# A two-layer diffusion trunk: 40 of 48 modulation units go from TensorE's matmuls to GpSimd's multiplies and sums

## The chip, the cores and the metric

The kernel runs on one core of a Trainium2 chip. The metric is the device time of one launch in microseconds (us), the median of some runs. An engine here is one of TensorE (PE in the profile, its weight loads PEld), VectorE (DVE), ScalarE (ACT), GpSimd (POOL) and SyncE (SP, which issues transfers). Each has its own in-order stream of instructions, and the streams meet only at semaphores: a `wait_ge(sem, n)` holds its own engine, and everything behind it on that engine, until the count is reached.

## The reference, cut to what matters

A layer takes 128 context tokens and 512 latent tokens, each with its own conditioning vector, and computes

```
m = silu(cvec) @ w_mod[l] + b_mod[l]                 # 1024 -> 6 x 1024, for 2 vectors
sh1, sc1, g1, sh2, sc2, g2 = split(m, 6)
h = rmsnorm(x) * (1 + sc1) + sh1
q, k, v, bg, cg, xc = split(h @ w_in[l])             # 1024 -> 3072
x = x + g1 * (concat(diff_attention(q, k, v), rmsnorm(bg * dwconv3(cg * xc))) @ w_out[l])
h2 = rmsnorm(x) * (1 + sc2) + sh2
a, b = split(dwconv3(h2 @ w_up[l]))                  # 1024 -> 2 x 2816
x = x + g2 * ((silu(a) * b) @ w_down[l])
```

for two layers. The change touches only the first line. Per layer it is a product of two vectors (context and latent) with a matrix of 1024 x 6144, 25 MB in float32, so its arithmetic is small and its weights are a third of a layer's. Of the results, sh1 and sc1 are wanted at the layer's start, g1 at the output projection, sh2 and sc2 in front of the MLP, g2 at the first down projection.

## The kernel before, in words

**Tokens.** All 640 tokens (with padding, T = 644 columns) pass together; large products are cut into two halves of 322 columns. Each float32 weight is split into a rounded part (`w_hi`, written by ScalarE) and a rest (`w_lo`, a subtraction by VectorE or, for one unit of each layer, GpSimd), and each product is three matmuls: hi x hi, hi x lo, lo x hi. Weights are staged in `raw_all` (nine blocks of 128x512), which SP fills in an order of units. Before, that order (`load_order`) interleaves weight units ("split") with modulation units ("mod").

**Stages of a layer.** (1) Norm and the products q, k, v, in six weight units (`qkv_unit`, loops p and t). (2) 24 "conv halves" (`conv_half`), with the 20 attention rounds between them: scores, the softmax on ScalarE and VectorE, transposes and the product with v, which goes to PSUM bank 7. (3) The output projection, four units (`out_unit`). (4) A gap: sums of squares (`stat`), root, reciprocal, spreading over the partitions (`spread`), the scaled rows `hfull`, and their split. (5) The MLP: 22 gates in four chunks. Two gates are plain; each other gate (`up_gate`) is seven products by a Strassen-like scheme, whose sums of weight blocks are made by GpSimd: three SBUF-to-SBUF transfers that add (`add_block`) and one `tensor_tensor` per gate. After each chunk comes its part of the down projection (`down_chunk`).

**Modulation before.** A unit is 1024 x 256 of `w_mod`. Its sum (`mod_sum`) is eight float32 matmuls: the eight inner tiles are spread over the four 32-column groups of the array, with `cT` (the activated vectors) stationary and the weights moving. Two units fill bank 7. ScalarE copies that to `mod_row` (`rows`), TensorE turns it by four transposes (`mod_turn`), VectorE sums the four groups and adds the bias (`mod_post`). There are 48 units: 8 (`pre_load`, `pre_sum`) are layer 0's sh1 and sc1 and are the same before and after; the other 40 are placed one by one between matmuls of q, k, v, of the output projection (layer 0 only) and in the two gaps. Those 40 end in 20 turns.

**GpSimd before** issues a few small loads and stores (`kc`, `v`, `rope`, new_k, new_v), and works only from the gap on: the subtraction for unit `G_U + 1` (line 680), six small `tensor_scalar` on `hfull` (line 685) and the sums for the gates (lines 668 and 698).

Of the kernel before, what the change touches and what calls it, by code (L numbers as in the profile page):

```python
# [15 lines left out]
P = 128  # L16
# [48 lines left out]
MOD_LAYER = 24  # L65
MOD_RING = MOD_LAYER - 8
RAW_SLOT = (N_SPLIT + MOD_RING) // 2
RAW_PRE = 0
MOD_PRE_G, MOD_LAYER_G = MOD_PRE // 2, MOD_LAYER // 2

# [8 lines left out]
GAP_A = [10] * LAST + [6]  # L79


def load_order(l):

    mod = [("mod", j) for j in range(MOD_LAYER)]
    split = [("split", n) for n in range(N_SPLIT)]
    order = split[0:4]
    for h in range(2, 6):
        order += mod[2 * h:2 * h + 2] + split[h + 2:h + 3]
    order += split[8:14]
    if l == LAST:  # L90
        return order + split[14:18]
    for h in range(6, 9):
        order += mod[2 * h:2 * h + 2] + split[h + 8:h + 9]
    return order + mod[18:20] + split[17:18]


ORDER = [load_order(l) for l in range(DEPTH)]


def raw_of(l, n):  # L100

    return ORDER[l].index(("split", n))
# [93 lines left out]
def mod_bank(l, h):  # L196

    return 2 if l is not None and h == GAP_A[l] + 1 else MOD_BANK


def sum_bank(l, h):

    return 4 if l and h == 1 else mod_bank(l, h)
# [5 lines left out]
def hybrid_step(nc, x_prompt, x_sample, cache_k, cache_v, c_sample, c_ctx, w_mod, b_mod, norm1_g, w_in, q_norm_g,  # L209
# [3 lines left out]
    with ctx:  # L213
# [28 lines left out]
        mod_row = sb("mod_row", [P, 2 * UC])  # L242
        qkg = sb("qkg", [P, 2, DEPTH, HD])
# [55 lines left out]
        early_gap = ExitStack()  # L299
        mod_t = sb("mod_t", [P, 2, SLOT], scope=early_gap)  # L300
        early_gap.close()
        ht_hi = sb("ht_hi", [P, KH, 3, HALF], F32R, scope=mlp)
        ht_lo = sb("ht_lo", [P, KH, 3, HALF], F32R, scope=mlp)
        gap = ExitStack()
        mod_x = sb("mod_x", [P, 2, SLOT], scope=gap)
        gap.close()
# [66 lines left out]
        modq_full, v_in = [sem("modq_full%d" % u) for u in range(4)], sem("v_in")  # L373
        modx_full, modt_full = sem("modx_full"), sem("modt_full")
# [31 lines left out]
        def landed(l, r):  # L406
            return 32 * (RAW_PRE + r % 2) + l * (32 * RAW_SLOT) + 32 * (r // 2)
# [6 lines left out]
        w_mod_v = w_mod.rearrange("l (t p) n -> p (l t) n", p=P)  # L414


        @block.sync
        def _(sp):
# [37 lines left out]
            def first_mods(layer, us):  # L456

                for u in us:
                    sp.dma_start(mod_q[:, u, :].rearrange("p (t n) -> p t n", n=UC),
                                 w_mod_v[:, layer * KT:(layer + 1) * KT, (u + 8) * UC:(u + 9) * UC]  # L460
                                 ).then_inc(modq_full[u], 16)

            for l in range(DEPTH):
                def free_of_split(n):
                    sp.wait_ge(split_full[n % 2], usable(l, n))

                def free_of_mod(k):
# [21 lines left out]
                def mod_source(j):  # L489

                    return (l, j + 8) if j < 16 else (l + 1, j - 16)

                def mod_unit(j, slot):

                    layer, unit = mod_source(j)
                    load(slot, w_mod_v, layer * KT, KT, unit * UC, UC)

                def gap_first():  # L500

                    sp.wait_ge(o_read, ROUNDS * (l + 1))
                    for i in range(2):
                        layer, unit = mod_source(2 * GAP_A[l] + i)
                        sp.dma_start(mod_t[:, i, :].rearrange("p (t n) -> p t n", n=UC),
                                     w_mod_v[:, layer * KT:(layer + 1) * KT, unit * UC:(unit + 1) * UC]
                                     ).then_inc(modt_full, 16)

                def gap_second():

                    sp.wait_ge(mix_ready, MIXN * (l + 1))
                    for i in range(2):
                        layer, unit = mod_source(2 * GAP_A[l] + 2 + i)
                        sp.dma_start(mod_x[:, i, :].rearrange("p (t n) -> p t n", n=UC),
                                     w_mod_v[:, layer * KT:(layer + 1) * KT, unit * UC:(unit + 1) * UC]
                                     ).then_inc(modx_full, 16)

# [3 lines left out]
                for r in range(2, len(ORDER[l])):  # L521
                    before, j = ORDER[l][r - 2]
                    if l or r not in (3, 4):
                        free_of_split(j) if before == "split" else free_of_mod(j + 1)
                    kind, n = ORDER[l][r]
                    if l == 0 and r == 3:
                        sp.wait_ge(mod_used, 6)
                        first_mods(0, (0, 1))
                    elif l == 0 and r == 4:
                        sp.wait_ge(mod_used, 8)  # L530
                        first_mods(0, (2, 3))
                    if l == LAST and (kind, n) == ("split", O_U + 2):
                        gap_first()
                    if kind == "mod":
                        if l == 0 and r == 4:
                            free_of_split(j)
                        mod_unit(n, r % 2)
# [1866 lines left out]
```

## Time and profile before

| | |
|---|---|
| three runs | 1579.79, 1579.90, 1580.26 us; median 1579.9 us |
| the profiled execution | span 1578.7 us from its first to its last instruction; the page gives no other time of that execution, so the 1.2 us to the median stand for what lies around it |
| TensorE busy | 1556.4 us, 99% |
| VectorE busy | 1046.2 us, 66% |
| ScalarE busy | 727.5 us, 46% |
| GpSimd busy | 187.3 us, 12%, none of it in 129 to 366 us, and two issues in 757 to 871 us |
| TensorE granted clock | 0.994 over the span |

A busy TensorE is a pipelined one: the durations of single matmuls overlap, so the cost of a matmul is the distance from start to start. The stages of layer 0 run from 0 to 145 us (loads, norm, q, k, v), to 299 (conv and attention), to 361 (output projection), to 372 (gap), to about 801 (MLP); layer 1 follows in the same form.

### The profile page before, as it was taken

How to read it: one execution, taken by the hardware profiler on the slowest of the kernel's cores; microseconds unless marked ns; L12 is line 12 of the kernel's file. 1: busy time of each engine (PE TensorE's matmuls, PEld its weight loads, DVE VectorE, ACT ScalarE, POOL GpSimd, SP SyncE). 2: the span in 40 equal slices, each digit the busy share in tenths (PEclk: the TensorE clock that was granted, in tenths of full speed). 3: DMA queues.
4: the chain of work that ended last, by engine and by line, in shares of the span. 5: the costliest groups of instructions: out<-in, count | busy, mean ns of one | idle time of the engine just before them, and what ended most of it. 6: DMA issues, size and time to landing. Idle time of an engine off the chain costs nothing. (4 is left out here: it accounts for less than half of the span.)

```text
span 1578.7 us, 26411 instructions
## 1 busy us (share of the span) xinstructions
PE 1556.4 (99%) x10573; PEld 1455.2 (92%) x10573; DVE 1046.2 (66%) x1661; ACT 727.5 (46%) x1218; POOL 187.3 (12%) x197
## 2 busy tenths in 40 slices
PE   8999999999999999999999999999999999999998
PEld 6677889988999999999987788899899999999998
DVE  6762666737875865857777547676588677486683
ACT  5433454326552633626444344542565355263461
POOL 1000000003211302212000000000222120130210
PEclk9999999999999999999999999999999999999999
DMA  9554010465755846658453621032357574584752
GB/s 361 202 180 165 28 54 28 161 197 157 177 133 153 200 128 158 163 146 194 142 180 108 202 79 54 28 108 91 111 138 170 134 186 122 152 195 130 181 140 84
DMA packets 278751, 225.64 MB, mean 143 GB/s; under 512 B 10058, under 2 KB 254084, under 8 KB 278628
## 3 DMA queue, kind: packets, MB, share of 16 engines
q1 hardware_dynamic: 260064, 189.89, 38.2%
q0 software_dynamic: 18320, 33.96, 12.5%
q8 instruction: 84, 1.38, 0.4%
q14 instruction: 39, 0.32, 0.1%
q10 hardware_dynamic: 244, 0.09, 0.0%
HBM read 188.78 MB, written 3.67 MB: 122 GB/s over the span
## 5 line engine op out<-in xcount | busy, mean ns | idle before, releaser
L1636 ACT ACTIVATE w_hi<-raw_all 128x1024 fp32r<-128x1024 f32 x120 | 126.4, 1058 | 205.6 <-PE ps L1245 100.0
L1243 PE MATMUL ps<-gg,w_hi 128*128 128x322 f32 x704 | 218.5, 310 | 0.0
L1245 PE MATMUL ps<-gg,w_lo 128*128 128x322 f32 x704 | 218.3, 310 | 0.0
L1244 PE MATMUL ps<-gg,w_hi 128*128 128x322 f32 x704 | 218.1, 310 | 0.0
L1188 PE MATMUL ps<-hc_lo,w_hi 128*128 128x322 f32 x640 | 199.5, 312 | 0.0
L1186 PE MATMUL ps<-hc_hi,w_hi 128*128 128x322 f32 x640 | 199.0, 311 | 0.0
L2233 DVE TENSOR_TENSOR w_lo<-raw_all,w_hi 128x1024 fp32r<-128x1024 f32 x120 | 149.1, 1243 | 74.8 <-ACT w_hi L1636 72.5
L1190 PE MATMUL ps<-hc_hi,w_lo 128*128 128x322 f32 x640 | 198.6, 310 | 0.0
L668 POOL DMA_DIRECT2D raw_all<-raw_all x120 | 102.8, 862 | 554.8 <-DMA raw_all<-in_w_up_dram 465.1
L2128 DVE SCALAR_TENSOR_TENSOR x<-ps,modv,x 128x128 f32<-128x128 f32 (+2 forms) x240 | 90.3, 433 | 91.8 <-PE ps L1245 54.5
L2194 DVE SCALAR_TENSOR_TENSOR tmp<-ub,vecs,tmp 128x642 f32<-128x642 f32 x168 | 140.8, 883 | 15.0 <-ACT tmp L1594 13.5
L1186 PE MATMUL ps<-ht_hi,w_hi 128*128 128x322 f32 x480 | 149.1, 311 | 1.1 <-ACT u L1654 1.0
L1190 PE MATMUL ps<-ht_hi,w_lo 128*128 128x322 f32 x480 | 148.5, 309 | 0.0
L1188 PE MATMUL ps<-ht_lo,w_hi 128*128 128x322 f32 x480 | 148.1, 309 | 0.0
L1243 PEld LDWEIGHTS ps<-gg,w_hi 128*128 128x128 f32 x704 | 132.6, 188 | 0.0
L1245 PEld LDWEIGHTS ps<-gg,w_lo 128*128 128x128 f32 x704 | 132.6, 188 | 0.0
L1244 PEld LDWEIGHTS ps<-gg,w_hi 128*128 128x128 f32 x704 | 132.4, 188 | 0.0
L1819 DVE TENSOR_TENSOR w_lo<-raw_all,w_hi 128x2048 fp32r<-128x2048 f32 x33 | 75.5, 2288 | 73.9 <-ACT w_hi L1347 73.9
L728 PE MATMUL ps<-h_hi,w_hi 128*128 128x322 f32 x384 | 123.6, 322 | 0.0
L1186 PEld LDWEIGHTS ps<-hc_hi,w_hi 128*128 128x128 f32 x640 | 120.7, 189 | 0.0
L1188 PEld LDWEIGHTS ps<-hc_lo,w_hi 128*128 128x128 f32 x640 | 120.6, 188 | 0.0
L1190 PEld LDWEIGHTS ps<-hc_hi,w_lo 128*128 128x128 f32 x640 | 120.6, 188 | 0.0
(236 smaller groups left out, 3551.7 us busy)
## 6 DMA issues: line engine op xcount, KB each, us to landing
raw_all<-in_w_up_dram SPq DMA_DIRECT2D x280, 256.0 KB, 4.1
raw_all<-raw_all POOLq DMA_DIRECT2D x120, 256.0 KB, 4.0
raw_all<-in_w_in_dram SPq DMA_DIRECT2D x48, 512.0 KB, 4.9
raw_all<-in_w_mod_dram SPq DMA_DIRECT2D x48, 512.0 KB, 4.3
raw_all<-in_w_down_dram SPq DMA_DIRECT2D x16, 768.0 KB, 4.3
raw_all<-in_w_down_dram SPq DMA_DIRECT2D x16, 640.0 KB, 4.1
mod_q<-in_w_mod_dram SPq DMA_DIRECT2D x8, 1024.0 KB, 9.4
raw_all<-in_w_out_dram SPq DMA_DIRECT2D x16, 512.0 KB, 4.3
```

The lines of the kernel that those rows point to most:

```text
L668: pool.dma_start(raw_f[:, BLK * dst:BLK * (dst + 1)], raw_f[:, BLK * src:BLK * (src + 1)], accum_op=ALU.add).then_inc(sum_full[which], 16)
L728: mm(out, wh[:, k, col:col + P], mov_hi(k), start=k == 0, stop=False)
L1186: mm(out, whi_f[:, c0:c0 + P], hh[:, k, slot, :], start=first and k == 0, stop=False, skip_group_check=not first)
L1188: mm(out, whi_f[:, c0:c0 + P], hl[:, k, slot, :], start=False, stop=False, skip_group_check=not first)
L1190: ins = mm(out, wlo_f[:, c0:c0 + P], hh[:, k, slot, :], start=False, stop=k == KH - 1, skip_group_check=not first)
L1243: mm(out, wh[:, k, :], gh, start=k == 0, stop=False)
L1244: mm(out, wh[:, k, :], gl, start=False, stop=False)
L1245: ins = mm(out, wl[:, k, :], gh, start=False, stop=k == kf - 1)
L1636: A(whi_b[:, 2 * i:2 * (i + 1), :], src, ACT.Copy).then_inc(up_hi[i], 1)
L2128: ins = V.scalar_tensor_tensor(out=xs, in0=ps[:, banks[h], p0:p0 + n], scalar=gate, in1=xs, op0=ALU.mult, op1=ALU.add)
L2194: return V.scalar_tensor_tensor(out=cen[:, s, 1:T - 1], in0=u[:, s, j:j + T - 2], scalar=vecs[:, l, w:w + 1], in1=cen[:, s, 1:T - 1], op0= ...
L2233: V.tensor_tensor(wlo_b[:, pair, :], raw_b[:, pair, :] if i else first_pair(g), whi_b[:, pair, :].bitcast(F32), ALU.subtract).then_inc(up_ ...
```

## The change

The 40 units become ten vectors of 1024 columns (`MODS`): layer 0's g1, sh2, sc2, g2; layer 1's sc1, sh1, then its g1, sh2, sc2, g2. Each is 16 steps on GpSimd (two column halves of 512, eight inner tiles). A step (`mod_step`) is:

- a transfer of 128x512 of `w_mod`, now issued by GpSimd (`mod_fetch`), two steps ahead, into `modw` or into block 8 of `raw_all` in turn. In the gates of layer 0 there is only `modw`, and the fetch is one step ahead;
- two `tensor_scalar` of 128x512: the tile times the context value and times the latent value of each partition (`cT[:, k, s]`);
- for all but the first tile of a half, one `tensor_tensor` of 128x1024 that adds both products to `moda`.

`moda` has one copy, so a vector's first step waits until TensorE has read the vector before it. TensorE sums `moda` over the partitions (`acc_sum`: four float32 matmuls of 512 columns with ones as a stationary 128x32), ScalarE copies the row, TensorE turns it (`acc_turn`: four float32 matmuls with four moving columns), and VectorE adds the bias (`acc_post`).

Four vectors of each layer are made by 64 steps ahead of the subtraction for `G_U + 1`; the other 32 steps (layer 1's sc1 and sh1) lie between the block sums of layer 0's gates: one in most gates, two behind gates 11 and 21, six behind gates 5 and 16, the latter ahead of the first block sum of the next chunk. TensorE takes the first vector of a layer in the v product (p = 2, t = 1), the second after conv half 8, the third after half 22, the fourth in the gap ahead of `spread`; layer 1's sc1 and sh1 within the down projections of chunks 1 and 3.

SP no longer loads modulation units between weight units; it takes over the small loads and stores of GpSimd, and waits for step 64 before it loads the block of the first gate that lies in block 8.

```diff
-def load_order(l):
-    mod = [("mod", j) for j in range(MOD_LAYER)]
-    split = [("split", n) for n in range(N_SPLIT)]
...
+MODS = [(0, v) for v in (2, 3, 4, 5)] + [(1, v) for v in (1, 0, 2, 3, 4, 5)]
+MOD_STEPS = 2 * KT
+GATE_STEPS = {1: 1, 2: 1, 3: 1, 4: 1, 5: 6, 7: 1, 8: 1, 9: 1, 10: 1, 11: 2,
+              12: 1, 13: 1, 14: 1, 15: 1, 16: 6, 17: 1, 18: 1, 19: 1, 20: 1, 21: 2}
+MOD_MID = {8: 1, 22: 2}
...
+            def mod_step(n):
+                m, h, k = n // MOD_STEPS, n // KT % 2, n % KT
+                pool.wait_ge(modw_full[mod_buf(n)], 16 * sum(mod_buf(j) == mod_buf(n) for j in range(n + 1)))
+                if k == 0 and h == 0 and m:
+                    pool.wait_ge(acc_used, m)
+                if n > k:
+                    pool.wait_ge(mod_added, (KT - 1) * (n // KT) + max(k - 1, 0))
+                elif k > 1:
+                    pool.wait_ge(mod_added, k - 1)
+                for s in range(2):
+                    out = moda[:, h, s, :] if k == 0 else modp[:, s, :]
+                    ins = nc.gpsimd.tensor_scalar(out, mod_w(n), cT[:, k, s:s + 1], 1.0, ALU.mult, ALU.mult)
+                ins.then_inc(modw_read, 1)
...
+                        mod_fetch(n + 1)
...
+                    mod_fetch(n + 2)
+                if k:
+                    pool.wait_ge(modw_read, n + 1)
+                    nc.gpsimd.tensor_tensor(moda[:, h, :, :], moda[:, h, :, :], modp[:, :, :], ALU.add
+                                            ).then_inc(mod_added, 1)
+            pool.wait_ge(cT_ready, 1)
+            pool.wait_ge(pre_full[7], 32)
...
-            def mod_sum(l, h, u, b, landed_at):
...
+            def acc_sum(m):
+                pe.wait_ge(mod_added, 2 * (KT - 1) * (m + 1))
...
+                for q in range(4):
+                    ins = mm(ps[QUAD * q:QUAD * (q + 1), MOD_BANK, 0:MW], ones[:, 0:QUAD], moda[:, q // 2, q % 2, :],
+                             start=True, stop=True)
+                ins.then_inc(acc_used, 1)
...
                         qkv_unit(0, t)
-                        pair_steps(2 * p, 0, t)
+                        if p == 2 and t == 1:
+                            acc_sum(first_mod(l))
...
                 stat(l, 2)
-                mod_sum(l, GAP_A[l], 0, "t", None)
+                acc_sum(first_mod(l) + 3)
                 spread(l, 2)
-                mod_sum(l, GAP_A[l], 1, "t", None)
-                for u in range(2):
-                    mod_sum(l, GAP_A[l] + 1, u, "x", None)
...
-                    if g != S_GATES[-1]:
+                    same = g != S_GATES[-1] and chunk_of(S_GATES[S_GATES.index(g) + 1]) == chunk_of(g)
+                    if same:
                         first_sum(S_GATES[S_GATES.index(g) + 1])
+                    if l < LAST:
+                        for n in range(mod_next, mod_next + GATE_STEPS[g]):
+                            mod_step(n)
+                        mod_next += GATE_STEPS[g]
+                    if not same and g != S_GATES[-1]:
+                        first_sum(S_GATES[S_GATES.index(g) + 1])
```

The streams themselves, as they are laid down. GpSimd ahead of the gates of layer 0, before (L651 to L664 are small transfers, L680 the subtraction for `G_U + 1`):

```order
L651 DMA rope<-in_rope_dram 128x512
L658 DMA kc<-in_cache_k_dram 128x512
L660 DMA v<-in_cache_v_dram 128x512
L662 DMA out_dram<-qn 128x512
L664 DMA out_dram<-v 128x512
L680 ISA
L680 TENSOR_TENSOR w_lo<-raw_all,w_hi 128x2048
L685 TENSOR_SCALAR hfull<-hfull,gain,modv 128x128 x6
```

And now, the first three of 64 steps (L592 is the fetch, L614 the two products, L624 the addition):

```order
L592 DMA modw<-in_w_mod_dram 128x512
L592 DMA raw_all<-in_w_mod_dram 128x512
L614 ISA
L614 TENSOR_SCALAR moda<-modw,cT 128x512 x2
L592 DMA modw<-in_w_mod_dram 128x512
L614 TENSOR_SCALAR modp<-raw_all,cT 128x512 x2
L592 DMA raw_all<-in_w_mod_dram 128x512
L624 TENSOR_TENSOR moda<-moda,modp 128x1024
L614 TENSOR_SCALAR modp<-modw,cT 128x512 x2
L592 DMA modw<-in_w_mod_dram 128x512
L624 TENSOR_TENSOR moda<-moda,modp 128x1024
```

64 such steps now stand ahead of the subtraction for `G_U + 1`. GpSimd in two gates of chunk 0, before (L668 are block sums by transfer, the third of three is the next gate's first; L698 is the block sum by instruction):

```order
L668 DMA raw_all<-raw_all 128x512 x3
L698 TENSOR_TENSOR raw_all<-raw_all 128x512
L668 DMA raw_all<-raw_all 128x512 x3
L698 TENSOR_TENSOR raw_all<-raw_all 128x512
```

And now (L639 and L669 are the same sums):

```order
L639 DMA raw_all<-raw_all 128x512 x2
L669 TENSOR_TENSOR raw_all<-raw_all 128x512
L639 DMA raw_all<-raw_all 128x512
L614 TENSOR_SCALAR modp<-modw,cT 128x512 x2
L592 DMA modw<-in_w_mod_dram 128x512
L624 TENSOR_TENSOR moda<-moda,modp 128x1024
L639 DMA raw_all<-raw_all 128x512 x2
L669 TENSOR_TENSOR raw_all<-raw_all 128x512
```

A step stands between the next gate's first block sum and its second. TensorE in the product v, p = 2, t = 1 (L889 is the last matmul of the tile, L758 one modulation unit, L985 four transposes of k), before:

```order
L887 MATMUL ps<-w_hi,h_hi 128x512
L888 MATMUL ps<-w_lo,h_hi 128x512
L889 MATMUL ps<-w_hi,h_lo 128x512
L758 MATMUL ps<-raw_all,cT 32x256 x8
L985 MATMUL ps<-ident,qn 128x128 x4
```

And now:

```order
L854 MATMUL ps<-w_hi,h_hi 128x512
L855 MATMUL ps<-w_lo,h_hi 128x512
L856 MATMUL ps<-w_hi,h_lo 128x512
L739 MATMUL ps<-moda,ones 32x512 x4
L930 MATMUL ps<-ident,qn 128x128 x4
```

The unit is replaced by the sum of a whole vector (four units' worth), and this one waits for GpSimd.

## Rows read from the trace of the kernel before

**Rows 1.** The page, part 1: busy us (share of the span) xinstructions.

```profile
PE 1556.4 (99%) x10573; PEld 1455.2 (92%) x10573; DVE 1046.2 (66%) x1661; ACT 727.5 (46%) x1218; POOL 187.3 (12%) x197
```

**Rows 2.** Waits of TensorE: us in total, times, longest.

```profile
PE ps L758 <- DMA raw_all<-in_w_mod_dram: 3.1, 4, 1.5
```

**Rows 3.** Timeline of TensorE, q, k, v of layer 0: start, us, what.

```profile
108.52 0.60 PE L771 MATMUL ps<-ident,mod_row 128*128 128x128 f32 x4
108.95 0.60 PE L985 MATMUL ps<-ident,qn 128*128 128x128 f32 x4
...
111.95 0.39 PE L889 MATMUL ps<-w_hi,h_lo 128*128 128x512 f32 x1
112.27 1.07 PE L758 MATMUL ps<-raw_all,cT 128*32 128x256 f32 x16
113.28 0.66 PE L985 MATMUL ps<-ident,qn 128*128 128x128 f32 x4
...
116.33 0.39 PE L889 MATMUL ps<-w_hi,h_lo 128*128 128x512 f32 x1
116.57 0.60 PE L985 MATMUL ps<-ident,qn 128*128 128x128 f32 x4
```

**Rows 4.** Timeline of TensorE, the gap of layer 0.

```profile
360.85 1.17 PE L785 MATMUL ps<-ones,ssq 128*128 128x1 f32 x10
...
363.78 1.94 PE L758 MATMUL ps<-mod_t,cT 128*32 128x256 f32 x16
```

**Rows 5.** Timeline of TensorE, the gap of layer 1.

```profile
1124.97 1.93 PE L758 MATMUL ps<-mod_t,cT 128*32 128x256 f32 x16
```

**Rows 6.** Two lines of GpSimd: duration ns min/median/max, first and last start.

```profile
L680 POOL TENSOR_TENSOR w_lo<-raw_all,w_hi x2: 4567/4568/4570, 366.0 to 1127.2; 128x2048 fp32r<-128x2048 f32 x2
...
L685 POOL TENSOR_SCALAR hfull<-hfull,gain,modv x12: 449/717/971, 370.6 to 1140.9; 128x128 f32<-128x128 f32 x12
```

**Rows 7.** Timeline of all engines at two moments: start, us, engine, line.

```profile
374.35 0.82 DVE L2177 TENSOR_TENSOR hc_lo<-hfull,hc_hi 128x644 fp32r<-128x644 f32 x1
...
374.52 0.97 POOL L685 TENSOR_SCALAR hfull<-hfull,gain,modv 128x128 f32<-128x128 f32 x1 [1.51 <-DVE hfull L2166]
...
421.51 1.29 POOL L698 TENSOR_TENSOR raw_all<-raw_all 128x512 f32<-128x512 f32 x1 [0.77 <-DMA raw_all<-raw_all]
...
421.95 1.54 DVE L2221 TENSOR_TENSOR gg<-gt,gg 128x644 fp32r<-128x644 f32 x1
```

**Rows 8.** Busy us (x instructions) in stretches of both layers.

```profile
46.00:361.00 315.00, 308.65 (x2117) 264.52 (x2113) 184.70 (x343) 126.60 (x272) 1.63 (x3) 0.99 0.38 126
768.00:1123.00 355.00, 354.07 (x2331) 314.34 (x2329) 228.18 (x421) 148.98 (x301) 2.26 (x4) 1.00 0.32 108
```

**Rows 9.** Groups of VectorE in 46 to 361: busy us, mean ns.

```profile
L1819 DVE TENSOR_TENSOR w_lo<-raw_all,w_hi 128x2048 fp32r<-128x2048 f32 x15 | 34.3, 2287 | 34.6 <-ACT w_hi L1347 34.6
...
L2032 DVE SCALAR_TENSOR_TENSOR probs<-probs,rec 128x640 f32<-128x640 f32 x16 | 14.1, 884 | 1.2
...
L2005 DVE TENSOR_TENSOR rt<-qraw,rope_q 128x512 f32<-128x512 f32 x8 | 5.5, 684 | 0.1
```

**Rows 10.** Transfers: KB each, median us from issue to landing.

```profile
kc<-in_cache_k_dram POOLq DMA_DIRECT2D x2, 256.0 KB, 5.2
```

**Rows 11.** Timeline of TensorE: the last units that are loaded ahead.

```profile
44.26 1.93 PE L758 MATMUL ps<-mod_q,cT 128*32 128x256 f32 x32
```

**Rows 12.** Timeline of GpSimd in layer 0's gates.

```profile
431.08 0.85 POOL L668 DMA_DIRECT2D raw_all<-raw_all  x1 [4.78 <-DMA raw_all<-in_w_up_dram]
...
478.60 0.86 POOL L668 DMA_DIRECT2D raw_all<-raw_all  x1 [29.07 <-DMA raw_all<-in_w_up_dram]
...
755.06 1.30 POOL L698 TENSOR_TENSOR raw_all<-raw_all 128x512 f32<-128x512 f32 x1 [0.94 <-DMA raw_all<-raw_all]
```

**Rows 13.** Timeline of ScalarE: the first weight pair of chunk 1.

```profile
495.76 1.06 ACT L1636 ACTIVATE w_hi<-raw_all 128x1024 fp32r<-128x1024 f32 x1 [9.16 <-PE ps L1245]
```

**Rows 14.** Busy us of all engines over one gate.

```profile
530.00:543.00 13.00, 13.00 (x90) 13.00 (x89) 10.59 (x13) 8.63 (x14) 4.25 (x5) 1.00 0.87 197
```

More of the change, by code:

```diff
@@ L193, with first_mod, turn_place @@
 PRE_SLOT = {0: 0, 4: 2, 1: 1, 5: 3, 2: 4, 6: 5, 3: 6, 7: 7}
[L196 to L203, printed above, removed]
+def first_mod(l):
+    return 6 * l
+def turn_place(m):
+    return (0, 3 * P) if m - first_mod(MODS[m][0]) == MOD_MID[8] else (MOD_BANK, 0)
 LAM_INIT = [0.8 - 0.6 * math.exp(-0.3 * i) for i in range(DEPTH)]
@@ L520, in _ @@
                     split_unit(1)
[L521 to L537, printed above, removed]
-                    elif n < G_U:
-                        if l == 0 and r == 3:
-                            free_of_split(j)
-                        split_unit(n)
-                    else:
-                        gate_unit(n % 2, CLASSIC[n - G_U])
-                    if l < LAST and (kind, n) == ("mod", 2 * 6 + 1):
-                        gap_first()
@@ L548, in free_of_slot0 @@
                 def free_of_slot0():
[L550 to L551 removed]
+                    free_of_split(G_U)
                 def block(b, row, half, g):
@@ L775, in stat, with pre_turn @@
-            def stat(l, which, between=None):
+                    for part in range(2):
+                        for q in range(4):
+                            k = 4 * part + q
+                            ins = mm(ps[QUAD * q:QUAD * (q + 1), MOD_BANK, u * UC:(u + 1) * UC], cT[:, k, :],
+                                     wu[:, k, :], start=part == 0, stop=part == 1)
+                    ins.then_inc(mod_used, 1)
+            def pre_turn(h):
+                pe.wait_ge(row_read, h + 1)
+                for t in range(4):
+                    ins = nc.tensor.transpose(ps[:, MOD_BANK, t * P:(t + 1) * P], mod_row[:, t * P:(t + 1) * P],
+                                              ident[:, :])
+                ins.then_inc(modT_full, 1)
@@ L777, in stat @@
+            def stat(l, which):
                 pe.wait_ge(ssq_ready, 3 * l + (1 + which))
                 for last, part in enumerate((ssq, sq)):
-                    if last and between:
-                        between()
                     if last and which != 1:
@@ L1275, in down_chunk @@
                         down(c, m, 0, kf)
+                        if l < LAST and c % 2 and m == 5:
+                            acc_sum(GATE_MODS[c // 2])
+                        elif l < LAST and c % 2 and m == 6:
+                            acc_turn(GATE_MODS[c // 2])
                 for c in range(len(CHUNKS)):
```

373 lines of the change are left out of this document (138 added, 235 removed).

## The prediction, written before the changed kernel had run

> **What bounds the kernel now.** I read the page's busy shares first: TensorE is busy for 99% of the span, VectorE for 66%, GpSimd for 12% [rows 1]. Then the waits of TensorE: the largest that belong to the modulation are four of 3.1 us together, for weights that had not landed [rows 2]. So time goes down if TensorE's stream gets shorter and nobody makes it wait. Then the timelines, for what the moved work costs there. One unit: from a last tile matmul to the transposes behind it are 1.33 us with a unit between (111.95 to 113.28) and 0.24 us without (116.33 to 116.57), so 1.09 us. One turn: 108.52 to 108.95, 0.43 us [rows 3]. Last I read what GpSimd and VectorE do to each other, because the new owner of the work is slow and starts late.
>
> **What TensorE saves.** Layer 0 up to the gap: 20 units x 1.09 = 21.8, ten turns x 0.43 = 4.3, the 3.1 of waits: 29.2 us. Added there: three sums and three turns. A sum is 8 records of 512 columns against a unit's 16 of 256; bounds are half a unit (if loads set the pace) and a whole one (if columns do), and I take 1.0 us. A turn is 8 records with full weight loads and next to no columns; ten such records of `stat` begin within 0.9 us [rows 4], so 0.8, with 0.4 (the old turn) as the lower bound. 3 x 1.8 = 5.4. Net 23.8: TensorE by itself would reach the fourth vector of layer 0 at 340 instead of 363.8 [rows 4]. The four units in each gap fill a wait for VectorE's scaled rows and give nothing. Layer 1: 8 units 8.7, five turns 2.2, about 2 of the four units at its start, minus 5.4: 7.5 us, so 1117.5 instead of 1125.0 [rows 5]. The rest (two sums in the down projections, four turns for four) costs 3, and VectorE's copy of a row in each gap gives 1. With no wait anywhere the sum would be 1580 - 24 - 7.5 + 2 = 1551.
>
> **What a step costs GpSimd.** The addition of 128x1024: 128x512 takes 1.29 us when nothing disturbs it [rows 7], 128x2048 takes 4.57 [rows 6], so 2.13 ns per column and 2.38 us. A product of 128x512 is not in the trace; the nearest row, 128x128, takes 0.45 undisturbed [rows 6]. Lower bound 0.45 (all of it fixed), upper 1.29 (the two-input form of the same width [rows 7]). If the fixed part is that of the addition, 0.2, the width gives 1.21. I take 1.0, twice. The issue of a fetch: 1.63 us for three issues of such transfers, so 0.54 [rows 8]. 0.2 for two waits on its own semaphores, my choice. Together 5.1 us, of which 4.4 with the tile in hand; with the ends of the product, 4.0 to 5.7. The landing (5.2 us [rows 10]) hides behind the step between. 64 steps: 328 us.
>
> The Trainium skill, GPSIMD Engine Reference, section 3.1 "Elementwise — side-by-side cycle accounting", gives 769 ns as measured for a tight one-input loop over 512 elements. No row here shows it. By it the step would be 4.65, and the whole sum below about 1695.
>
> **What VectorE adds to that.** In the row at 421.95 VectorE's 128x644 with two SBUF inputs takes 1.54 us, beginning 0.44 into GpSimd's addition; the same form takes 0.82 at 374.35. GpSimd's ends at 422.80, and 422.80 + 0.82 is nearly the 423.49 at which VectorE's ends. The other way round, GpSimd's product takes 0.97 instead of 0.45 behind VectorE's instruction of 374.35, which ends at 375.17 [rows 6, 7]. So each waits for the whole of the other's instruction. VectorE has 116 us of such instructions between 46 and 361: nine groups, from 34.3 down to 5.5 [rows 9], are 94, smaller ones about 22; 148 instructions. Not all of it lengthens GpSimd: some 0.3 us of each is dispatch that overlaps, and GpSimd holds for 4.4 of 5.1 us. (116 - 44) x 0.87 = 63 us, with bounds of 0 and 116. Layer 1 by VectorE's busy time, 228 against 185 [rows 8]: 78, bounds 0 and 142.
>
> The Trainium skill, SBUF — State Buffer, section "SBUF: two separate sides", says the same: the port pair that VectorE and GpSimd share is an exclusive lock, held for a whole instruction by a GpSimd instruction or by a VectorE one with two SBUF inputs. It speaks against moving this work. By a shared bandwidth without a lock the sum would be the second rival's, by the lock it is the forecast.
>
> **Layer 0.** The steps begin when the last preloaded unit is there, at 44.3 at the latest since TensorE then sums it [rows 11], and a fetch of 5.2 has landed [rows 10]: between 45 and 49.5, I take 47. The first vector is wanted at 112.3 before, less 8 units and 4 turns: 102. Sixteen steps are 82 us, and VectorE's q and k norms in this stretch add 19: 148. TensorE waits 46 us in the v product. Since GpSimd is then never ahead, it sets every later meeting point too (half 8, half 22, gap); TensorE's and VectorE's own work lies in its shadow. Fourth vector: 47 + 328 + 63 = 438, against 363.8: +75 us. TensorE's saving is swallowed. The gap behind is as before.
>
> **Layer 0's gates.** Six-step places: GpSimd is idle from 449.5 to 478.6 [rows 12], but ScalarE reads the first sum only at 495.8 [rows 13], so with some 5 us for the transfer the limit is 490, 41 us. With one buffer a step lasts 2.0 + 5.2 = 7.2, six of them 43 less the first landing, 38, plus 10 of VectorE's: 8 us late, twice: 16. One-step places: GpSimd waits 4.8 us there now [rows 12], about a step, so its chain is delayed by 2 to 3 us, which the double buffering bears. But VectorE works 10.6 of 12.4 us per gate [rows 14]; with 4.4 us more in which it is shut out it needs 14.7, and its subtraction for a bank that TensorE wants in the same gate is in that queue. 2.3 us x 12 gates (the first of each chunk's four has little on VectorE) = 28. Together 44, bounds 0 and 90.
>
> **Layer 1.** The last block sum of layer 0 ends at 756.4 [rows 12]; two gate steps of 5.1 and 7.2 less overlap, and a fetch: 774 on the old clock. 774 + 328 + 78 = 1180 against 1125.0: +55 us. Its gates have no steps and stay.
>
> **Sum.** 1578.7 + 75 + 44 + 55 + 2 (turns and sums behind the last meeting) = 1755, plus 1.2 to the median: **1756 us**. Removed waits of ScalarE and VectorE are worth nothing, since both get more idle time. TensorE's clock may fall to its lower level in waits of tens of us; where GpSimd is the limit this costs nothing more.
>
> **Rivals.**
> 1. *GpSimd nearly keeps up.* The product takes 0.5 to 0.6 us and the holds cost next to nothing, as VectorE's instructions fall in gaps. Step 4.2, 64 of them 269: done at 316 and 1043, ahead of 340 and 1117. Only the first vector is late, 47 + 67 = 114 against 102. 1551 + 12 = 1563. For it: GpSimd's idle stretches in gates and chunks have the length of one and of six such steps. Against it: rows 7, and the trend of rows 6.
> 2. *Long steps, cheap holds.* 5.1 a step: layer 0 at 375, +11; layer 1 at 1102, hidden, -7.5; gates 0: 1585. For it: 0.87 of VectorE's time might fall into issues and waits. Against it: VectorE is busy 59% of 46 to 361.
> 3. *The lock bites in full.* Product 1.2, extension 85%: step 5.5, 352. Layer 0: 47 + 352 + 99 = 498, +134; layer 1: 774 + 352 + 121 = 1247, +122; gates 60: 1896. For it: VectorE, late, keeps its whole chain (scores, softmax, split) waiting, and TensorE reaches its own work late in each stretch between meeting points. It is the forecast's mechanism at a higher price.
>
> Rival 1 turns into the forecast from a step of about 4.7 us, holds included, in layer 0 (340 less 47, over 64 = 4.6).
>
> **Chances.** Forecast 0.60, rival 3 0.23, rival 2 0.08, rival 1 0.09. Range: all ends together give 1563 to about 1960; leaving out a tenth at each side I give 1630 to 1900. What three runs can tell from no change is about 0.2%, 3 us: faster 0.09, same 0.02, slower 0.89.
>
> **What the new profile should show.** TensorE's waits led by the line of `acc_sum`, four long ones in each layer's first part, the first some 46 us in the v product; GpSimd busy nearly without a break from 47 to about 438 and again through layer 1's first half, near 80% of those stretches or more; its addition with a minimum of 2.4 and a higher mean, its product near 1.0; VectorE's two-input groups (the 128x2048 split, 2.29 now) with longer means; gates of layer 0 at about 14.7 us, of layer 1 at 12.4. Wrong are the forecast's sizes if the product's minimum is under 0.6 or the means stand at the minima; wrong is its mechanism if TensorE waits at `acc_sum` for less than 20 us in all.

## The result and the profile after

The changed kernel takes **1761.7 us** (median of four, 1756.37 to 1763.47) against 1579.85 (median of four, 1578.84 to 1580.26) for the kernel before in the same comparison: **1.1151 times as long, 95% interval 1.1134 to 1.1167**. The forecast was 1756 in a range of 1630 to 1900. The profiled execution has a span of 1759.3 us, 180.6 more than before.

Part 1 of its page, the answer to [rows 1]:

```profile
PE 1585.9 (90%) x10013; PEld 1483.8 (84%) x10013; DVE 1331.0 (76%) x1629; ACT 725.3 (41%) x1210; POOL 959.1 (55%) x808
```

TensorE has 560 instructions fewer and is busy 29 us longer, VectorE has 32 fewer and is busy 285 us longer. GpSimd has 772 us more. The waits of TensorE (us in total, times, longest), the answer to [rows 2], and below them one of GpSimd's:

```profile
PE ps L988 <- DVE probs L1941: 39.9, 23, 4.4
PE ps L739 <- POOL moda L624: 24.8, 3, 12.3
PE ps L1110 <- ACT u L1571: 14.0, 9, 2.0
PE ps L973 <- ACT probs L1400: 13.9, 12, 1.7
...
PE ps L1086 <- DVE hc_lo L2080: 7.8, 2, 3.9
```

```profile
POOL moda L614 <- PE ps L739: 111.2, 6, 27.6
```

L739 is `acc_sum`, L988 the transposes of the attention weights, L973 the scores, L1110 a product of a gate, L1086 the plain gates; L614 is the first product of a new vector. TensorE waits longest for the end of VectorE's softmax, not for GpSimd's vectors, and GpSimd waits 111.2 us for TensorE to take a vector: in the middle of each layer it is ahead, not late.

Where the 180 us are, by TensorE's first matmul of each stage:

| stage | layer 0: before, after | layer 1: before, after |
|---|---|---|
| q, k, v | 123.8, 138.0 (+14.1) | 103.7, 118.8 (+15.1) |
| conv and attention rounds | 137.5, 181.1 (+43.6) | 137.5, 179.5 (+42.0) |
| output projection | 77.6, 71.2 (-6.5) | 65.1, 66.9 (+1.8) |
| gap | 11.0, 20.2 (+9.2) | 11.5, 24.4 (+13.0) |
| MLP, to the next layer or the end | 434.6, 482.1 (+47.5) | about -1 |

The head of layer 1 adds 1.3; by these marks layer 0's MLP ended at 806.5 before, not at about 801. Busy time in four stretches, columns span, TensorE, weight loads, VectorE, ScalarE, GpSimd, TensorE's granted clock, DMA share, GB/s: the rounds of layer 0, its gap, and two of its gates, the second and the fourth of a chunk's five:

```profile
160.10:341.20 181.10, 154.26 (x974) 136.18 (x974) 145.01 (x162) 66.37 (x178) 125.71 (x104) 0.93 0.24 75
...
412.40:432.60 20.20, 7.26 (x42) 5.16 (x41) 10.07 (x18) 7.20 (x10) 15.57 (x11) 0.60 0.23 66
```

```profile
598.10:610.90 12.80, 12.70 (x86) 12.43 (x85) 12.80 (x13) 8.16 (x12) 9.28 (x7) 1.00 0.90 208
625.20:639.80 14.60, 12.64 (x85) 12.38 (x85) 14.60 (x14) 8.16 (x12) 11.48 (x10) 1.00 0.45 124
```

Before, the same rounds took 137.5 us with 92.9 of VectorE and the clock at 1.00. In the gate of 14.6 us VectorE is never idle; before, it worked 10.6 us in the 13.0 of [rows 14], and as much in the 12.4 of the gate that lies in them (531.1 to 543.5).

Groups of VectorE after (busy us, mean ns, idle before):

```profile
L2097 DVE SCALAR_TENSOR_TENSOR tmp<-ub,vecs,tmp 128x642 f32<-128x642 f32 x168 | 191.3, 1188 | 14.0 <-ACT tmp L1511 13.4
...
L1734 DVE TENSOR_TENSOR w_lo<-raw_all,w_hi 128x2048 fp32r<-128x2048 f32 x33 | 95.6, 2896 | 46.3 <-ACT w_hi L1274 45.9
...
L1938 DVE TENSOR_TENSOR rec<-rec,neglam 128x1 f32<-128x1 f32 x40 | 48.9, 1222 | 3.0
L1970 DVE TENSOR_REDUCE mx<-ps 128x2 f32<-128x1280 f32 x32 | 47.4, 1482 | 5.6 <-PE ps L973 5.5
...
L1973 DVE TENSOR_SCALAR nbias<-mx 128x2 f32<-128x2 f32 x40 | 42.1, 1054 | 3.1
...
L1941 DVE SCALAR_TENSOR_TENSOR probs<-probs,rec 128x640 f32<-128x640 f32 x32 | 39.1, 1223 | 2.4
...
L1936 DVE RECIPROCAL rec<-sums 128x2 f32<-128x2 f32 x40 | 6.6, 164 | 39.3 <-ACT probs L1400 38.6
```

Before, these means were 883, 2288, 159, 1490, 169, 885 and 165 ns. The product of one number per partition with another (`rec`) takes 7.7 times as long, the scaling of two numbers (`nbias`) 6.2 times. The maximum over scores, which reads PSUM, and the reciprocal keep their length. `rec`, `nbias` and the 128x640 form of `probs` together grow by 42.5 + 35.3 + 10.8 = 88.6 us; the rounds of both layers grew by 85.6. That these are near each other proves nothing: experiment 6 takes most of this growth away, and the rounds get back less than a third of theirs.

What one such moment looks like, on all engines:

```profile
263.12 0.57 POOL L592 DMA_DIRECT2D modw<-in_w_mod_dram  x1 [0.71 <-POOL modp L614]
263.72 2.40 POOL L624 TENSOR_TENSOR moda<-moda,modp 128x1024 f32<-128x1024 f32 x1
263.76 1.49 DVE L1970 TENSOR_REDUCE mx<-ps 128x2 f32<-128x1280 f32 x1
...
265.32 0.83 DVE L1973 TENSOR_SCALAR nbias<-mx 128x2 f32<-128x2 f32 x1
...
266.19 0.79 ACT L1400 ACTIVATE probs<-ps,nbias 128x640 f32<-128x640 f32 x1 [0.78 <-DVE nbias L1973]
```

GpSimd's addition ends at 266.12, `nbias` at 266.15, and ScalarE's exponential, the next link, begins at 266.19. The reduction runs beside the same addition at its usual 1.49. Of the 80 `rec` and `nbias` instructions 48 are stretched (longer than 0.3 us), and 46 of them end within 0.04 us of the end of an addition or a product of GpSimd.

GpSimd's own lines, duration ns min/median/max, the answer to [rows 6]:

```profile
L614 POOL TENSOR_SCALAR modp<-modw,cT x152: 681/939/3124, 51.0 to 1298.8; 128x512 f32<-128x512 f32 x152
L614 POOL TENSOR_SCALAR modp<-raw_all,cT x128: 682/874/2954, 46.2 to 1302.7; 128x512 f32<-128x512 f32 x128
...
L624 POOL TENSOR_TENSOR moda<-moda,modp x140: 2337/2400/4078, 48.5 to 1303.5; 128x1024 f32<-128x1024 f32 x140
```

### The profile page after: what moved, and what is told of

Same layout as the page of the kernel before. It is cut to its first block, busy times and chain, and to the rows that moved or that the text cites. A ratio compares the mean times of both kernels' runs of the same rounds, so it can differ in the third digit from the quotient of the medians.

```text
span 1759.3 us, 25937 instructions
## 1 busy us (share of the span) xinstructions
PE 1585.9 (90%) x10013; PEld 1483.8 (84%) x10013; DVE 1331.0 (76%) x1629; ACT 725.3 (41%) x1210; POOL 959.1 (55%) x808
## 3 DMA queue, kind: packets, MB, share of 16 engines
q8 instruction: 79, 1.29, 0.3%
## 4 chain that ended last, share of the span: by engine, by line
PE 32%; DVE 9%; POOL 4%; DVEq 2%; ACT 2%; issue 1%; ACTq 0%; POOLq 0%
PE ps L1110 5%; PE ps L1112 5%; PE ps L1114 5%; PE ps L1167 3%; PE ps L1169 3%; PE ps L1168 3%; POOL moda L624 2%; POOL modp L614 2%; DVE rec L1938 1%; DVE nbias L1973 1%; DVE w_lo L1734 1%; DVE probs L1941 1%; PE ps L854 1%; PE ps L855 1%; PE ps L856 1%
## 5 line engine op out<-in xcount | busy, mean ns | idle before, releaser
L624 POOL TENSOR_TENSOR moda<-moda,modp 128x1024 f32<-128x1024 f32 x140 | 340.0, 2429 | 3.9
L639 POOL DMA_DIRECT2D raw_all<-raw_all x120 | 103.7, 882 | 414.9 <-DMA raw_all<-in_w_up_dram 384.9
L1110 PE MATMUL ps<-hc_hi,w_hi 128*128 128x322 f32 x640 | 201.0, 314 | 6.7 <-DVE ub L2159 6.6
L2097 DVE SCALAR_TENSOR_TENSOR tmp<-ub,vecs,tmp 128x642 f32<-128x642 f32 x168 | 191.3, 1188 | 14.0 <-ACT tmp L1511 13.4
L2136 DVE TENSOR_TENSOR w_lo<-raw_all,w_hi 128x1024 fp32r<-128x1024 f32 x120 | 155.5, 1296 | 60.5 <-ACT w_hi L1553 59.4
L614 POOL TENSOR_SCALAR modp<-modw,cT 128x512 f32<-128x512 f32 x152 | 160.7, 1074 | 21.6 <-DMA modw<-in_w_mod_dram 12.6
L1110 PE MATMUL ps<-ht_hi,w_hi 128*128 128x322 f32 x480 | 150.2, 313 | 14.3 <-ACT u L1571 14.0
L1167 PEld LDWEIGHTS ps<-gg,w_hi 128*128 128x128 f32 x704 | 134.0, 190 | 10.8 <-DVE gg L2124 7.3
L614 POOL TENSOR_SCALAR modp<-raw_all,cT 128x512 f32<-128x512 f32 x128 | 133.8, 1054 | 9.1 <-POOL moda L624 8.4
L704 PE MATMUL ps<-h_hi,w_hi 128*128 128x322 f32 x384 | 131.6, 343 | 0.0
L1734 DVE TENSOR_TENSOR w_lo<-raw_all,w_hi 128x2048 fp32r<-128x2048 f32 x33 | 95.6, 2896 | 46.3 <-ACT w_hi L1274 45.9
```

Of the source, the lines that this page charges most:

```text
L614: ins = nc.gpsimd.tensor_scalar(out, mod_w(n), cT[:, k, s:s + 1], 1.0, ALU.mult, ALU.mult)
L624: nc.gpsimd.tensor_tensor(moda[:, h, :, :], moda[:, h, :, :], modp[:, :, :], ALU.add).then_inc(mod_added, 1)
L704: mm(out, wh[:, k, col:col + P], mov_hi(k), start=k == 0, stop=False)
L1110: mm(out, whi_f[:, c0:c0 + P], hh[:, k, slot, :], start=first and k == 0, stop=False, skip_group_check=not first)
L1167: mm(out, wh[:, k, :], gh, start=k == 0, stop=False)
L2097: return V.scalar_tensor_tensor(out=cen[:, s, 1:T - 1], in0=u[:, s, j:j + T - 2], scalar=vecs[:, l, w:w + 1], in1=cen[:, s, 1:T - 1], op0= ...
```

## The experiments

All start from the changed kernel. Theories: **lock** (VectorE's instructions wait for GpSimd's, and the loss runs through VectorE's chains), **deadline** (TensorE waits for vectors that come too late), and, for the first, fetches, queue order or clock by themselves. "Before" was 1579 to 1580 in every comparison.

**1. Fetches alone (e1).** `mod_step` without arithmetic:

```
-                for s in range(2):
-                    ... tensor_scalar(out, mod_w(n), cT[:, k, s:s + 1], ...)
-                ins.then_inc(modw_read, 1)
+                pool.sem_inc(modw_read, 1)
...
-                    nc.gpsimd.tensor_tensor(moda[:, h], moda[:, h], modp, ALU.add).then_inc(mod_added, 1)
+                    pool.sem_inc(mod_added, 1)
```

> The changed kernel with GpSimd's products and adds left out: it still fetches all 160 tiles, in the same order, and gives the same semaphores; TensorE sums a constant buffer. Lock theory (VectorE waits out GpSimd's instructions): with them the whole loss goes, and what is left is TensorE's saving: 1551 us (the all-hidden sum), between 1545 and 1565; rec x neglam and nbias back at 0.16 us. Deadline theory (TensorE waits for GpSimd's vectors): the same 1551. Third theory (the fetches on GpSimd's queue, SyncE's new order, or TensorE's clock cost the time): it stays over 1650.

Measured: 1566.0 us (1564.2 to 1567.3), ratio 0.9912, interval 0.9896 to 0.9928. `rec` and `nbias`:

```profile
L1972 DVE TENSOR_SCALAR nbias<-mx 128x2 f32<-128x2 f32 x40 | 6.9, 172 | 3.0
...
L1937 DVE TENSOR_TENSOR rec<-rec,neglam 128x1 f32<-128x1 f32 x40 | 6.4, 159 | 3.0
```

So 196 us hang on GpSimd's arithmetic; fetches, SyncE's new order and the missing units are together a small gain. It is 15 above the 1551: by the marks of the stage table, layer 0's MLP takes 449.3 instead of 434.6, 3.8 of it for two vectors. Held against e1 instead of the kernel before, the changed kernel loses 79.3 us in the rounds, 52.0 in q, k, v, 32.8 in layer 0's MLP, 21.7 in the gaps and 8.9 in the output projections. So q, k, v are the second largest part. Up to its first vector TensorE waits there mostly for `kT` (ScalarE, 5.9 us) and for VectorE's `h_lo` and `w_lo` (5.2 and 4.8); no run takes this part further apart.

**2. Nobody waits for the vectors (e2).**

```
-                pe.wait_ge(mod_added, 2 * (KT - 1) * (m + 1))
+                pe.wait_ge(rope_full, 16)
...
-                    ins = mm(..., ones[:, 0:QUAD], moda[:, q // 2, q % 2, :], ...)
+                    ins = mm(..., ones[:, 0:QUAD], rope (a settled table, 128x512), ...)
```

> The changed kernel, but TensorE's acc_sum reads a fixed table and waits for no vector; GpSimd does all its work as before. Lock theory: only TensorE's waits at acc_sum (24.8 us in three) can go, and part of them comes back: 1735 to 1760 us, the attention rounds still 40 us longer per layer than before the change. Deadline theory: the late vectors are the cause, so 100 us or more come back: under 1660.

Measured: 1754.3 us (1752.1 to 1758.8). The 24.8 us of waits at `acc_sum` are gone, and 7 of them come off the time. The rounds are 175.4 and 179.0 us. The 7 us are a net figure: the two gaps are 13.8 us shorter and the rounds 6.2, but q, k, v of layer 0 and the MLP of layer 1 are 7.1 and 7.3 longer, though the edit changes nothing in GpSimd's or VectorE's work. Single stretches thus shift by some 7 us with the moments at which the two engines meet. Late vectors are not the cause of this kernel's loss.

**3. Work left out in one place or of one kind (e5, e6, e7).** e5 drops the arithmetic of the steps in layer 0's gates, e6 the additions everywhere, e7 the products.

> GpSimd's products and adds are left out for the two units of steps that stand among layer 0's gates (its fetches and semaphores stay). Lock theory: layer 0's MLP goes back from 482 us to about 430 (434.6 before the change, less the modulation units that left it): 1710 to 1720 in all; the attention rounds keep their 43 us. If the gates' loss is from fetches in the step's places or from TensorE's clock after the gap, it stays over 1740.

> The adds (128x1024, 2.4 us each) are left out, the products (128x512, 0.68 us) stay. Lock theory: a step is 2.2 us with no instruction over 0.7 us, so 1590 to 1640, rec x neglam 0.3 to 0.5 us. If the count of GpSimd's instructions and not their length decides, two thirds of the loss stays: about 1690.

> The products are left out, the adds stay. Lock theory: the add is the longest instruction and 2.4 of the 4.8 us of a step, so it carries most of the loss: 1650 to 1710, rec x neglam still near 1.2 us while GpSimd works. If the products matter as much: under 1650.

Measured: e5 1721.4 us (1716.7 to 1723.6), e6 1575.6, e7 1677.4 (one run each for the last two). In e5 the MLP of layer 0 takes 443.5 us:

```profile
433.60:877.10 443.50, 441.25 (x2969) 438.13 (x2969) 310.94 (x414) 216.37 (x300) 108.69 (x126) 1.00 0.65 169
```

VectorE is back at 311 us there, from 392. So the gates' share is 40 us, near what the lock theory has, though the stage does not fall to 430 and the time lies just above the expected 1710 to 1720. Products alone cost 9.6 us over e1, additions alone 111, both 196; why both together cost 75 more than their sum is not shown. For the products that is less than expected (the 1575.6 lie below the 1590 to 1640). Busy time does not explain that: GpSimd is busy 307 us more than in e1 with the products and 362 more with the additions. A product there has a minimum of 0.68 us and an addition 2.34, and `rec` and `nbias` have means of 259 and 268 ns beside products, 871 and 602 beside additions.

**4. Shorter instructions (e3).**

```
-                    ... tensor_scalar(out[512 columns]) ; tensor_tensor(128x1024)
+                    for c in range(0, MW, CUT):        # CUT = 256
+                        ... tensor_scalar(out[:, c:c + CUT], ...) ; tensor_tensor(... c:c + CUT ...)
```

> Each product in two of 128x256 and each add in four of 128x256: the same work, GpSimd's longest instruction 0.6 to 0.7 us instead of 2.4. Lock theory: a short VectorE instruction waits at most 0.7 us: rec x neglam and nbias fall from 1.22 and 1.05 us to 0.4 to 0.6, the attention rounds lose 20 to 30 of their 43 us per layer: 1660 to 1710. Deadline theory: GpSimd's steps get no shorter (a fixed cost on twice and four times as many), so the time stays at 1760 or grows.

Measured: 1842.6 us (1839.2 to 1846.4), the slowest of all, far from the lock theory's 1660 to 1710. Part of it is the deadline: 115 us of waits at `acc_sum` (88.6, and 26.8 for which the trace shows no releaser), since 560 additions of 0.71 us or more cost 422.5 us where 140 cost 340. But the holds should have become short, and did not: `nbias` has a mean of 1.11 us. One moment:

```profile
273.82 0.57 POOL L593 DMA_DIRECT2D raw_all<-in_w_mod_dram  x1 [0.30 <-POOL modp L616]
274.07 3.21 DVE L1979 TENSOR_SCALAR nbias<-mx 128x2 f32<-128x2 f32 x1
274.42 2.82 POOL L629 TENSOR_TENSOR moda<-moda,modp 128x256 f32<-128x256 f32 x4
```

`nbias` ends at 277.28, behind the last of four additions (277.24). Of 32 `rec` and `nbias` longer than 0.3 us that end with one of four additions 28 end with the fourth. My lock theory was wrong in one point: VectorE mostly did not get in between two additions that follow each other without a break.

**5. A break between two additions (e9, e10).** Both make the addition as two of 128x512; e10 alone has the marked line:

```
+                    for s in range(2):
+                        if s:                                                         # e10 only
+                            pool.wait_ge(half_added, (KT - 1) * (n // KT) + k)         # e10 only
+                        tensor_tensor(moda[:, h, s], moda[:, h, s], modp[:, s], ALU.add) ...
```

> The add of 128x1024 is made as two of 128x512, one right behind the other. Two forms of the lock theory. Run form (a VectorE instruction gets in only when a run of GpSimd instructions without a break between them has ended; the narrow kernel showed waits of 3.2 us beside four adds of 0.7 us): nothing is won, rec x neglam and nbias keep 1.0 to 1.2 us, the time is 1760 to 1785. Instruction form (it waits for the running one only): both fall to 0.6 to 0.8 us, the time to 1725 to 1750.

> As the kernel with two adds of 128x512, but the second waits on a semaphore that the first gives, so that there is a break of some 0.1 to 0.2 us between them. Run form: VectorE gets in at the break, rec x neglam and nbias fall to 0.6 to 0.8 us, and the time lies 15 to 35 us under that kernel's. Instruction form: both kernels alike, this one at most 5 us slower by the longer step.

Measured: 1774.4 us (1772.7 to 1779.9) without the break, 1739.0 (1734.7 to 1742.9) with it: 35 us for one wait that GpSimd does on itself. `rec` and `nbias` without it, then with it:

```profile
L1940 DVE TENSOR_TENSOR rec<-rec,neglam 128x1 f32<-128x1 f32 x40 | 56.1, 1402 | 3.0
...
L1975 DVE TENSOR_SCALAR nbias<-mx 128x2 f32<-128x2 f32 x40 | 35.6, 891 | 3.1
```

```profile
L1977 DVE TENSOR_SCALAR nbias<-mx 128x2 f32<-128x2 f32 x40 | 29.8, 746 | 3.1
...
L1942 DVE TENSOR_TENSOR rec<-rec,neglam 128x1 f32<-128x1 f32 x40 | 25.8, 646 | 3.0
```

Where the stretched ones end says the same: in e9 all 40 that stood behind a pair of additions end with the second one, in e10 31 of 43 end with the first. The run form is borne out for additions. Between two products VectorE did get in (in e3 11 of the 14 longer than 0.22 us that ended with one of four products did not wait for the last). The Trainium skill, SBUF — State Buffer, section "SBUF: two separate sides", has the lock taken for one instruction; here the measurement goes further, a run of additions counts as one.

**6. VectorE's short instructions taken out of the way (e4, e8).** e4 gives them to ScalarE, e8 only lets `nbias` read PSUM:

```
e4  -  V.tensor_scalar(nbias, mx, -SCALE, ...)          +  A(nbias, mx, ACT.Copy, scale=-SCALE)
    -  V.tensor_tensor(rec1, rec1, neglam, ALU.mult)    +  A(sums1, sums1, ACT.Copy, scale=1/neglam)
e8  -  mx = sb("mx", [P, 2, 2])                         +  mx = ps[:, 4, 300:304]
```

> nbias is formed by ScalarE, and the factor neglam is put on the sum by ScalarE before VectorE's reciprocal, so that VectorE's two shortest instructions go (91 us busy now, 13 before). Lock theory: 1690 to 1730, the attention rounds shorter by 15 to 35 us a layer, since each round has two fewer instructions that wait for GpSimd's. Deadline theory: 1755 to 1765, since GpSimd's vectors come no earlier.

> The maxima lie in PSUM instead of SBUF: the instruction that makes nbias (128x2) now reads PSUM; nothing else changes. Lock theory in the form that the trace suggests (only instructions with all operands in SBUF wait; those that read PSUM keep their length): nbias falls from 1.05 us back to 0.17 to 0.25, and the time by 10 to 35 us, to 1727 to 1750. If any VectorE instruction beside GpSimd waits: nbias stays at 1 us and the time at 1762.

Measured: e4 1742.4 us (1741.1 to 1749.7), e8 1740.0 (1736.4 to 1741.7). In e8:

```profile
L1973 DVE TENSOR_SCALAR nbias<-ps 128x2 f32<-128x2 f32 x40 | 6.4, 159 | 3.1
```

None of the 40 is stretched, beside the same GpSimd: with its source in PSUM the instruction doesn't wait, and this one line is worth 22 us; the rounds, 165.4 and 169.6, are 25.6 us shorter. In e4 two instructions a round are gone, but the next in line takes over a part of their wait: `probs` 128x640 goes from 1223 to 1500 ns and its product from 568 to 1080. So e4 gains 19, not the 32 to 72 of its expectation: 77.8 us of growth are gone and the rounds (167.3 and 168.8) get 24.5 back, while q, k, v of layer 0, which the edit does not touch, take 147.4 in the profiled execution.

**7. The additions on the DMA engines (e11).**

```
-                    nc.gpsimd.tensor_tensor(moda[:, h], moda[:, h], modp, ALU.add)
+                        pool.dma_start(moda[:, h, s, :], modp[:, s, :], accum_op=ALU.add).then_inc(mod_acc[s], 16)
```

> The adds go to the DMA engines: each product of 128x512 is added into the vector by an accumulating DMA (two of 256 KB a step) that GpSimd issues; GpSimd has no two-input instruction left in a step. The result is the reference's. Lock theory: only the products hold VectorE, which cost 10 us with the adds left out (1575.6 against 1566.0), so 1575 to 1600, if the steps (two products 1.4, three issues 0.57 to 0.86, waits: 4 to 5 us) still end in time; under 1579 it beats both kernels. Deadline theory: a step as long as now or longer gives 1750 or more. If the 280 transfers crowd out the weight loads: over 1600, with TensorE waiting for split units or gates.

Measured: 1740.8 us (1737.1 to 1746.2, five runs). VectorE is nearly free (1080.9 us busy, `rec` 277 ns), and the time is lost all the same. TensorE's waits, and the q, k, v stretch of layer 0:

```profile
PE ps L738 <- issue: 81.8, 4, 33.9
PE ps L738 <- DMA moda<-modp: 26.0, 2, 13.5
PE ps L1109 <- ACT s L1570: 22.5, 13, 4.9
```

```profile
22.20:167.70 145.50, 106.19 (x552) 82.14 (x552) 73.36 (x136) 49.10 (x77) 85.63 (x105) 0.87 0.81 209
```

L738 is `acc_sum` here. For 81.8 us the trace shows no releaser; I put them down to the same transfers, which no run shows: the instruction is the same, and in the longest of these waits, 34 us in the stretch above, GpSimd is busy and the DMA share is 0.84. GpSimd's fetches land after 4.3 to 4.6 us instead of 3.0. GpSimd spends 247.6 us on 280 issues (0.88 each) and waits 110 us for their landings. This is the deadline: the additions no longer hold VectorE, but the step is longer, and the vectors come late. The measured time lies between the two theories, 1575 to 1600 and 1750 or more.

**8. Both remedies (e12).** The break of e10 and the moved instructions of e4.

> Both remedies at once: the add in two of 128x512 with a break between them, and VectorE's two shortest instructions moved to ScalarE. Each alone gave 1739.0 and 1742.4, 23 and 19 us under the changed kernel. If VectorE's holds in the attention rounds are what is left: 1715 to 1725 (nearly the sum of both), those rounds 150 to 160 us. If TensorE's wait for the vectors takes over (it rose from 24.8 to 52 us when the break made GpSimd's step longer): 1730 to 1740, with more than 50 us of waits at acc_sum.

Measured: 1741.1 us (1736.0 to 1744.2), no better than e10 alone and just above the 1730 to 1740 of its second case. The waits at `acc_sum` are 59 us:

```profile
PE ps L744 <- POOL moda L629: 46.1, 3, 21.7
PE ps L993 <- DVE probs L1951: 23.1, 22, 2.3
PE ps L744 <- issue: 12.9, 2, 6.4
```

The second constraint is now the first: the deadline was hidden behind VectorE's delays, and appears once these are shortened. No version that does the whole work came under the kernel before, and e1 shows the most that could be had, 14 us.

| kernel | us | GpSimd's longest run without a break | rounds, layer 0 / 1 | waits at acc_sum |
|---|---|---|---|---|
| before | 1579.9 | | 137.5 / 137.5 | |
| e1, no arithmetic | 1566.0 | | 140.6 / 140.7 | 0 |
| e6, products | 1575.6 | 2 x 0.68 | 143.4 / 143.6 | 0 |
| e7, additions | 1677.4 | 2.34 | 158.2 / 158.6 | 0 |
| after | 1761.7 | 2.34 | 181.1 / 179.5 | 24.8 |
| e9, two additions | 1774.4 | 2 x 1.26 | 181.0 / 183.1 | 24 |
| e10, with a break | 1739.0 | 2 x 0.68 or 1.26 | 164.6 / 170.4 | 52 |
| e11, DMA adds | 1740.8 | 0.68 | 157.3 / 157.6 | 108 |
| e3, narrow | 1842.6 | 4 x 0.71 | 188.8 / 189.2 | 115 |

## Why the prediction was right, and where it was not

**The size and the mechanism's name.** 1756 against 1761.7. That VectorE and GpSimd shut each other out was read from two rows [rows 7] and is what e1, e8 and e10 show. The parts come out near as well: up to the first gate of layer 0 +61 (forecast +75), layer 0's MLP +47.5 (+44), layer 1 without its MLP +73 (+55).

**Who loses by it.** Here the forecast failed. It priced the lock as an extension of GpSimd's work (63 and 78 us) that delays vectors, with VectorE's own work "in its shadow". The extension is there and smaller: GpSimd's products and additions exceed their minima by 51 us in the first 64 steps and by 50 in the last 64. The overlap of 0.3 us an instruction that it took off had no row named; [rows 7] give 0.13 each way. It is the other way round: TensorE waits for VectorE's chain. The step that failed is "since GpSimd is then never ahead, it sets every later meeting point too". The fourth vector of layer 0 was ready at 424 (forecast 438), when TensorE had waited for it since 416 and not since 340. The vectors of the middle were ready first; TensorE waited at `acc_sum` three times, 4.4 us in the v product (forecast 46), 8.1 and 12.3 in the gaps. e2 puts the price of all deadlines at 7 us net, 13.8 in the gaps. By the test that I set, under 20 us in all, the mechanism stands at 24.8, just above; by e2 it doesn't stand. That the sum is right nonetheless is partly luck: the rounds' 86 us and the delays in q, k, v were not in it, and late vectors that did not occur stood in their place. Rival 3 named the right chain ("VectorE, late, keeps its whole chain waiting") but only as an aggravation.

**Why I missed it.** I weighed VectorE's instructions by busy time: the 128x2048 split first, and `rec` and `nbias`, 13 us together in the whole kernel, were below the nine groups of [rows 9]. But a hold costs what is left of GpSimd's run, whatever the length of the held instruction. What counts is how many held instructions stand in a chain that TensorE waits for: in a round `nbias`, `rec` and the two instructions on `probs` behind it.

**The step of GpSimd.** The product takes 0.68 us undisturbed, not the 1.0 I took; the bounds 0.45 to 1.29 held. The 769 ns of the Trainium skill (GPSIMD Engine Reference, section 3.1 "Elementwise — side-by-side cycle accounting") were nearer than my value. The addition's 2.38 is right (minimum 2.34, median 2.40). Fetch issue 0.57 (0.54). The landing is 3.0 us, not 5.2. The engine stands idle for 0.5 us around a step's waits, not 0.2. So the undisturbed step is some 4.8 us instead of 5.1, and GpSimd starts at 43.9 instead of 47.

**TensorE's saving.** From its first matmul to what follows, a sum takes 1.00 and a turn 0.81 us where TensorE doesn't wait (1.0 and 0.8 forecast). With all arithmetic hidden e1 gives 1566, not 1551: up to the first gate of layer 0 it saves 25.6 (24 forecast), in layer 1 up to its gates 4.0 (7.5), and layer 0's MLP costs 14.7 (3), of which the sums and turns are 3.8. The other 11 stand where only fetches and semaphores are left in GpSimd's queue; what they hold up was not taken apart.

**Gates.** The total is near (47.5 against 44), the parts are not. The later gates of the first two chunks last 12.8 to 15.0 us, layer 1's 12.4 to 12.7; the row of the gate of 14.6 us shows VectorE saturated, as the forecast had it from [rows 14]. Its working had two slips: those 10.6 us stand in a row of 13.0 us, and 10.6 + 4.4 are 15.0, not 14.7. Over the 16 gates that another one follows the growth is 18 us, where 28 were forecast: the second gate of a chunk grows by only 0.1 to 0.4 after the first chunk. The stretches from a chunk's last gate to the next chunk take 61.3, 61.2 and 57.3 us, and in e5, without the arithmetic, 55.0, 57.1 and 47.9. The first and the third have a six-step place, and they lose 2.2 and 5.3 us more than the second, where 8 each were forecast.

**TensorE's clock.** The forecast gave it no price. Its granted clock is 0.93 in the rounds and 0.60 in the gap (before 1.00 and 0.84), so TensorE runs partly at the lower level of 1.2 GHz there, after waits of up to 2.9 us in these rounds and 8.1 in the gap: just behind the gap its matmuls begin 0.27 us apart instead of 0.15. For the same 10013 instructions it is busy 1585.9 us, and 1529.7 in e1. Up to 56 of the 196 us are thus the echo of the waits in the clock; how many of them lie on the critical path no run separates.

## What to carry to other kernels

Before moving elementwise work to GpSimd, look for VectorE instructions with all operands in SBUF (of these the reciprocals and a reduction were never stretched here) that stand in a chain the bottleneck engine waits for, and count them instead of adding up their time: each may wait for a whole unbroken run of GpSimd's two-input instructions. If the work must be there, break GpSimd's runs with a wait, let short VectorE operands come from PSUM, and then see which deadline appears next.

## What the runs showed of the hardware that I had not expected

- A one-element VectorE instruction can take 2.8 us beside GpSimd (0.16 alone); `nbias` with its source in PSUM took 0.16 beside the same load, all 40 times. RECIPROCAL with operands in SBUF wasn't stretched either (164 ns against 165), nor was a reduction of 128x512 in SBUF (684 against 685). The groups that read PSUM kept their means within 3% (the 80 of 128x320 that update `x`: 542 ns before and after), while `tensor_tensor` from SBUF went up to 7.7 times its mean.
- GpSimd's hold covers back-to-back additions: 3.21 us beside four of 0.71; one wait of GpSimd on its own semaphore opened it (e9 against e10, 35 us).
- A hold seems to reach back over a DMA issue when an addition is queued behind it. In the changed kernel 14 of `rec` and `nbias` began during an issue. Of the 11 with an addition behind the issue, ten began 0.38 to 0.43 us ahead of the addition and lasted 2.80 to 2.83 us, to its end; the eleventh began 0.56 us ahead and took 0.17. The three with a product behind it took 0.16 to 0.37:

```profile
193.86 0.57 POOL L592 DMA_DIRECT2D modw<-in_w_mod_dram  x1 [0.30 <-POOL modp L614]
194.04 2.80 DVE L1938 TENSOR_TENSOR rec<-rec,neglam 128x1 f32<-128x1 f32 x1
194.46 2.35 POOL L624 TENSOR_TENSOR moda<-moda,modp 128x1024 f32<-128x1024 f32 x1
```

  In e1, with the same issues and nothing behind them, the seven `rec` and `nbias` that began in one lasted 0.16 to 0.26. Whether the issue or the queued addition holds VectorE was not tried.
